# A two-layer decoder step on one core: the recurrence in another order and in other PSUM banks, and the first norm's root multiplied in behind the projection

## The chip, the cores and the metric

The kernel runs on one core of a Trainium2 chip. The time is device microseconds from the start of one execution to its end. Three runs of the kernel before took 1614.56 to 1616.03 us, with a median of 1615.8. The profile is of one further execution, which took 1614.58 us.

## What is computed

The reference runs two decoder layers for 512 prompt tokens and 8 sample tokens (520 columns in all, 1024 features). The change touches the first half of layer 0:

```python
proj = rms_norm(x, norm_g) @ w_in            # 1024 -> 3600 columns
qkv, gdn_conv = causal_conv(g_qkv, ...)      # width 4, then silu; the same for x/B/C of the SSD heads
q, k = l2_normalize(q), l2_normalize(k)
beta = sigmoid(g_b);  g = -exp(A_log) * softplus(g_a + dt_bias)      # the gates
# chunks, 4 delta-rule heads:
lower = strict(kb @ k.T * decay);  u, w = solve(eye + lower, [v*beta, kb*exp(cum)])
v_new = u - w @ S;  o = (q*exp(cum)) @ S + (q @ k.T * decay) @ v_new
S = S * exp(last) + (k * exp(last - cum)).T @ v_new
# chunks, 8 SSD heads:  scores = C B^T * seg;  y = scores @ x + (C * exp(cum)) h;  h updated likewise
```

rms_norm multiplies each token by the inverse root of its mean square, and each feature by a gain. Behind the recurrence follow a second norm, the output projection, an FFN, and layer 1 (latent attention with a paged cache, and another FFN). These are as they were.

## The kernel before

**Layout.** Everything lies with features on the 128 partitions and tokens along the row, so x is 8 tiles of 128 x 520 (`xres`). Large products are done with the operands split in two parts, high and low: of the activations `xnh` and `xnl`, of the weights `wsplit` halves made by ScalarE (`high`, L1126) and VectorE (`low`, L1563) from a ring of four slots that SP fills, 512 KB each. An output tile takes for each of 8 feature tiles six matmuls of 260 columns (high with high, high with low, low with high, in two column halves). Tiles go to two pairs of PSUM banks in turn (0 and 1, 2 and 3). `gemm_ready` says that a tile is done, `tile_taken` that it has been read out, and the tile after the next one waits for that and for its weights (`w_split`).

**Start.** SP issues x in two DMAs, the page table, and then the weights. GpSimd issues the constants (1280 KB), the gains and six small tensors. When x and the page table are there, ScalarE squares the 8 tiles (L1109), VectorE adds them (L1518, L1521), TensorE sums over partitions (`norm_sum`), ScalarE makes the inverse root with an Ln and an Exp (L1113, L1115). Then for each tile VectorE forms the normalized x (`xraw`, L1617), ScalarE copies its high part (L1197), VectorE takes the low part (L1621), and TensorE follows tile by tile.

**Projection.** 28 output tiles in 7 turns of four. The first 20 go through the convolution. For each, ScalarE makes the high half of the weights of the tile after next, copies the tile from PSUM (L1207, two small copies for the outputs behind it) and, after VectorE's convolution, applies SiLU (L1215). VectorE makes the low half, then one multiply (L1633) and three rounds of multiply-add (L1636, L1638). Turn 0 stands by itself and turns 1 to 4 are a loop on every engine. Each engine runs its list in order, so a SiLU that waits for the convolution also holds ScalarE's next high half. After turn 0 TensorE does the gates: 40 matmuls of 16 columns from the normalized x and `wgate`, which VectorE and ScalarE turn into decays with about 15 small operations. The last 8 tiles (z) are copied out by ScalarE (L1246) into `hid`, between the lengths of q and k. ScalarE then applies SiLU to all eight z tiles in one operation (L1260).

**Recurrence.** Four chunks of 128 tokens. TensorE's list for a chunk: 12 decay sums broadcast over partitions into banks 0 to 2 (`cumB_mm`; 4 delta heads, 8 SSD heads), beta (bank 3), key-key (4), key-query (5), transposes of k (6) and v (7), then for the SSD part B-C products (0) and transposes of x (1) and B (2), then the first mask product transposed (3, `xinit_mm`). ScalarE makes exponentials of the sums (L1269, L1270). VectorE waits for them, subtracts each token's own sum (12 operations, L1699), waits for ScalarE's exponential (L1272), forms `bm` and `lt` (L1704, L1707), `attnt` (L1709), `xinvt` and `xinv` (L1711, L1713) and the scaled k and v (L1716 to L1719, `kvs_ready`). GpSimd multiplies `lt` with 7 masks (L435), each for one level of the inversion. Six levels follow: two products `y` (one for each half of the heads, copied by ScalarE, L1282), and two products that VectorE subtracts from `xinv` and `xinvt` (L1758, L1760). After level 0 VectorE does the SSD scores and the two state queries `ce` (L1726 to L1733); TensorE's SSD outputs behind level 1 wait for both. After the levels come `w_mm` (copied by ScalarE, L1284), `vnew_mm` (L1286), the outputs and the state products, and VectorE's state update (L1769). In the trace these transposes and matmuls appear as one or two records each, nearly all under the helper's line L505.

Of the kernel before, what the change touches and what calls it, by code (L numbers as in the profile page):

```python
# [57 lines left out]
INV_BANKS = ((3, 4, 5), (6, 7, 2))  # L58
# [12 lines left out]
SMALLS = ['w_gate', 'gains', 'convw', 'convb', 'small', 'gatec', 'prev']  # L71
# [32 lines left out]
def build(nc, A, O):  # L104
    ctx = ExitStack()
    with ctx:
# [22 lines left out]

        xraw = hid[:, 20:28]  # L130
# [142 lines left out]
        spt = sqsum[:, 0:256]  # L273
        rqs, qr, krn = sb("rqs", 128, 4, MH), sb("qr", 128, ROUNDS, 32), sb("krn", 128, ROUNDS)
# [7 lines left out]
        def unit(n):  # L282
# [3 lines left out]
        x_loaded, c_loaded, g_loaded = sem("x_loaded"), sem("c_loaded"), sem("g_loaded")  # L286
# [13 lines left out]
            w_mm w_ready qe_ready vnew_ready ot_mm ot_taken kv_mm s_ready bc_mm xtm_mm btm_mm score_ready  # L300
            xdt_ready btm_ready ce_ready yt_mm yt_taken hup_mm h_ready rec_stored st_loaded
            sprep_ready spread_mm spread_ready rhs2_ready sv_mm vnt_ready qks_mm row_mm row_ready
            sel_mm sel_taken y0_mm xds_ready hsel_mm hsel_taken s_decayed osq_ready osq_mm
            mix_ready dve_own h0_loaded ln_ready rinv_ready big_stored out_stored
            w_hi w_split part_done xn_raw xn_hi hid_hi hid_ready mix_split silu_ready up_ready
# [45 lines left out]
        def _(sp_):  # L351
            for k in range(2):
                sp_.dma_start(xres[:, 4 * k:4 * k + 4], A['x'][:, 4 * k:4 * k + 4]).then_inc(x_loaded, 16)
            sp_.dma_start(ptab[:, :], A['page_table']).then_inc(x_loaded, 16)
# [9 lines left out]

            def pages():

                sp_.wait_ge(x_loaded, 48)
# [14 lines left out]
            for stage, turns, _ in STAGES:  # L382
                for u in range(4):
# [4 lines left out]
                    load(stage, 0, u)  # L388
# [21 lines left out]
        def _(pool):  # L410
            pool.dma_start(cst[:, :, :], A['consts']).then_inc(c_loaded, 16)
            for dst, src in zip((wgate, gains, convw, convb, small, gatec, prev), SMALLS):
                pool.dma_start(dst[:], A[src]).then_inc(g_loaded, 16)
# [68 lines left out]
            pool.wait_ge(x_loaded, 48)  # L482
# [20 lines left out]
        def _(pe):  # L503
# [9 lines left out]
            def split_gemm(stage, high, low, begin=0, end=None, norm=None, after=None, ready=None):  # L513
# [45 lines left out]
            def norm_sum(n):  # L559
                pe.wait_ge(s('sq_added'), (KD - 1) * (n + 1))  # L560
# [5 lines left out]
            pe.wait_ge(c_loaded, 16)  # L566
            norm_sum(0)

            split_gemm('proj', xnh, xnl, 0, 1, norm=0)

            pe.wait_ge(g_loaded, 16 * len(SMALLS))
# [36 lines left out]
            for c in range(NCH):  # L608
# [14 lines left out]
                if c:  # L623
                    pe.wait_ge(s('x_ready'), 2 * LV * c)
# [1615 lines left out]
```

## Time and profile before

| | |
|---|---|
| median of 3 runs | 1615.8 us |
| profiled execution | 1614.58 us, its span 1612.9 us |
| busy: TensorE / its weight loads | 1526.5 us (95%) / 1424.2 us (88%) |
| busy: VectorE / ScalarE / GpSimd | 743.0 us (46%) / 604.6 us (37%) / 159.6 us (10%) |
| mean granted TensorE clock | 0.97 |
| chain that ended last, by engine | TensorE 89%, VectorE 5%, ScalarE 3% |

Start to 34 us is the norm and the first tile, to 209 us the projection, to 397 us the four chunks. In the rows, times are microseconds from the start of the span, the second figure is the time that the piece or instruction takes, and brackets hold the engine's idle time ahead of it with what ended it. A granted clock of 1.00 is 2.4 GHz and of 0.50 is 1.2 GHz.

### The profile page before, as it was taken

To read this page: it belongs to the slowest core of one execution; us is meant where nothing else is said; L and a number is where in the kernel's file an instruction comes from. 1 tells how busy PE (TensorE), PEld (TensorE's weight loads), DVE (VectorE), ACT (ScalarE), POOL (GpSimd) and SP (SyncE) were. 2 spreads that over 40 slices of the span, in tenths; PEclk is the share of its full clock that TensorE was granted. 3 is DMA by queue.
4 is the path that set the end of the run, shared out by engine and by line. 5 is a ranking of instruction groups with operands and counts; after the bars stand their busy time and mean duration, and the time that the engine had idled before them with its cause. 6 is when DMAs were issued, how large, how long until landed. Compare 5 with 4: busy or idle time off the path is not lost.

```text
span 1612.9 us, 29294 instructions
## 1 busy us (share of the span) xinstructions
PE 1526.5 (95%) x11912; PEld 1424.2 (88%) x11912; DVE 743.0 (46%) x1243; ACT 604.6 (37%) x934; POOL 159.6 (10%) x192
## 2 busy tenths in 40 slices
PE   4999978888799999999999999999899999999999
PEld 4999977777588999999999967677799999999998
DVE  5577346565574444444323425455434444444222
ACT  4454632221523443442222363456524443442111
POOL 1000022211160000000010000252111000000000
PEclk9999989898899999999999999999889999999999
DMA  5223200002134323333332322264322323332332
GB/s 185 68 80 103 69 11 1 1 1 104 49 77 162 90 89 94 91 90 104 91 95 78 96 78 79 71 179 145 131 79 81 92 90 92 92 90 89 94 95 76
DMA packets 46274, 140.27 MB, mean 87 GB/s; under 512 B 6706, under 2 KB 16018, under 8 KB 45042
## 3 DMA queue, kind: packets, MB, share of 16 engines
q1 hardware_dynamic: 39842, 114.38, 23.5%
q0 software_dynamic: 6064, 20.60, 4.3%
q10 hardware_dynamic: 288, 4.19, 0.7%
q8 instruction: 54, 0.88, 0.2%
q14 instruction: 26, 0.21, 0.0%
HBM read 130.34 MB, written 7.76 MB: 86 GB/s over the span
## 4 chain that ended last, share of the span: by engine, by line
PE 89%; DVE 5%; ACT 3%; issue 1%; DMA 1%; POOL 0%; SPq 0%; DVEq 0%; ACTq 0%
PE PS L505 88%; PE PS L971 1%; DVE arena L1699 1%; DMA ptab<-in_page_table 1%; DVE arena L1726 0%; POOL arena L435 0%; DVE arena L1617 0%; ACT rinv L1113 0%; DVE xnl L1621 0%; DVE sqsum L1521 0%; ACT arena L1452 0%; ACT arena L1260 0%; DVE arena L1760 0%; DVE arena L1955 0%; ACT sq L1319 0%
## 5 line engine op out<-in xcount | busy, mean ns | idle before, releaser
L505 PE MATMUL PS<-xnh,wsplit 128*128 128x260 f32 x3904 | 637.5, 285 | 7.0 <-DVE xnl L1621 4.4
L505 PEld LDWEIGHTS PS<-xnh,wsplit 128*128 128x128 f32 x3904 | 541.2, 190 | 9.3 <-issue 7.7
L505 PE MATMUL PS<-xnl,wsplit 128*128 128x260 f32 x1952 | 394.6, 284 | 0.0
L1126 ACT ACTIVATE wsplit<-wring 128x1024 fp32r<-128x1024 f32 x176 | 182.8, 1041 | 464.3 <-PE PS L505 457.9
L1563 DVE TENSOR_TENSOR wsplit<-wring,wsplit 128x1024 fp32r<-128x1024 f32 x176 | 211.0, 1201 | 247.1 <-ACT wsplit L1126 247.0
L505 PEld LDWEIGHTS PS<-xnl,wsplit 128*128 128x128 f32 x1952 | 302.3, 190 | 0.0
L505 PE MATMUL PS<-arena 128*128 128x128 f32 (+4 forms) x1328 | 209.3, 329 | 24.7 <-DVE arena L1699 5.6
L505 PE MATMUL PS<-hidh,wsplit 128*128 128x260 f32 x1408 | 226.6, 283 | 0.0
L505 PEld LDWEIGHTS PS<-arena 128*128 128x128 f32 (+2 forms) x1328 | 173.7, 207 | 58.2 <-issue 24.5
L505 PEld LDWEIGHTS PS<-hidh,wsplit 128*128 128x128 f32 x1408 | 192.9, 188 | 0.0
L505 PE MATMUL PS<-hidl,wsplit 128*128 128x260 f32 x704 | 141.3, 282 | 0.0
L505 PEld LDWEIGHTS PS<-hidl,wsplit 128*128 128x128 f32 x704 | 108.7, 188 | 0.0
L1577 DVE TENSOR_TENSOR sq<-PS,rinv 128x520 f32<-128x520 f32 x44 | 30.8, 700 | 119.9 <-PE PS L505 119.9
L1582 DVE TENSOR_TENSOR sgate<-PS,rinv 128x520 f32<-128x520 f32 x44 | 30.8, 700 | 119.3 <-PE PS L505 105.6
L505 PE MATMUL PS<-sq,cst 128*128 128x260 f32 (+1 forms) x184 | 51.7, 416 | 7.6 <-ACT sq L1319 6.7
L1126 ACT ACT_TABLE_LOAD x24 | 30.8, 1283 | 70.2 <-PE PS L505 70.1
L1282 ACT ACTIVATE arena<-PS 128x256 f32<-128x256 f32 x48 | 18.5, 384 | 92.0 <-PE PS L505 91.4
L435 POOL TENSOR_TENSOR arena<-arena,cst 128x512 f32<-128x512 f32 x28 | 36.3, 1329 | 166.9 <-DVE arena L1707 166.9
L505 PEld LDWEIGHTS PS<-sq,cst 128*128 128x128 f32 (+1 forms) x184 | 27.6, 164 | 22.3 <-ACT sq L1319 10.0
L422 POOL TENSOR_TENSOR sqsum<-sqsum,sq 128x520 f32<-128x520 f32 x18 | 32.9, 1826 | 126.2 <-ACT sq L1109 125.8
L1638 DVE SCALAR_TENSOR_TENSOR arena<-arena,convw 128x512 f32<-128x512 f32 x60 | 44.8, 747 | 0.0
L1452 ACT ACTIVATE arena<-PS,nb,rqs 128x512 f32<-128x512 f32 (+1 forms) x64 | 38.8, 628 | 1.9 <-DVE nb L2005 1.9
(356 smaller groups left out, 1645.9 us busy)
## 6 DMA issues: line engine op xcount, KB each, us to landing
wring<-in_w_gu SPq DMA_DIRECT2D x88, 512.0 KB, 3.6
wring<-in_w_dn SPq DMA_DIRECT2D x32, 512.0 KB, 3.5
wring<-in_w_proj SPq DMA_DIRECT2D x28, 512.0 KB, 3.6
wring<-in_w_dn SPq DMA_DIRECT2D x16, 384.0 KB, 3.2
wring<-in_w_outa SPq DMA_DIRECT2D x8, 512.0 KB, 3.7
wring<-in_w_inc SPq DMA_DIRECT2D x8, 512.0 KB, 3.6
wring<-in_w_uq SPq DMA_DIRECT2D x8, 512.0 KB, 4.8
wring<-in_w_outc SPq DMA_DIRECT2D x8, 512.0 KB, 3.8
```

Source lines behind the costliest of these rows:

```text
L422: pool.tensor_tensor(sqsum[:, :], sqsum[:, :], sq[:, k % 2, :], ALU.add).then_inc(s('sq_added'), 1)
L435: pool.tensor_tensor(by(mt[:, l], GH), by(lt, GH), across(const(f'inv{l}'), GH), ALU.mult)\
L505: return pe.matmul(out, lhsT, rhs, start=start, stop=stop)
L971: ins = pe.transpose(PS[:, bank(h, e), at_:at_ + 128], pm[:, PLACE[q] + kb * 128:PLACE[q] + (kb + 1) * 128], ident)
L1126: act.activation(dst[:, 0:w], wring[u][:, 0:w], ACT.Copy).then_inc(s('w_hi'), 1)
L1282: act.activation(yinv[:, hs_], PS[:, by_, hs_], ACT.Copy).then_inc(s('y_ready'), 1)
L1452: ins = act.activation(pm[:, to:to + w], PS[:, b0 + e, at_:at_ + w], ACT.Exp, bias=nb[:, q:q + 1], scale=rqs[:, q, h:h + 1], accum_out=den ...
L1563: tt(wl[:, 0:w], wring[u][:, 0:w], wh[:, 0:w].bitcast(F32), ALU.subtract).then_inc(s('w_split'), 1)
L1577: tt(two(supt), bank2(2), two(root), ALU.mult).then_inc(tile_taken[1], 1)
L1582: tt(two(sgate[:, q, :]), bank2(0), two(root), ALU.mult).then_inc(tile_taken[0], 1)
L1638: st(stt(out=cacc[:, p, 0:T], in0=raw[:, p, t:t + T], scalar=w(t), in1=cacc[:, p, 0:T], op0=ALU.mult, op1=ALU.add), s('conv_done') if t == ...
L1699: st(stt(out=arg[:, h // 4, hs_], in0=PS[:, h // 4, hs_], scalar=cumt[:, c, h:h + 1], in1=const('decaymask'), op0=ALU.subtract, op1=ALU.mi ...
```

## The change

**First norm.** x comes in four DMAs with a semaphore each, the first weights right behind the first of them, and the page table goes to GpSimd's list. GpSimd issues the gains first and the constants and small tensors only when the second quarter of x is there. ScalarE makes `xnh` as x times the gain, squares between, and VectorE makes `xnl` (`gained_low`) with the adds of the squares between. `norm_sum(0)` stands behind tile 0 on TensorE. Its root goes to `sqsum`, and VectorE multiplies with it as it reads each of the 28 tiles out of PSUM; ScalarE's copies of them are gone and its two small output copies read `raw`. The gates take raw x with `wgate` times the gain, and five matmuls of one column turn the root for them, which VectorE multiplies in.

**Recurrence.** The decay sums are in two groups, the four delta heads first. VectorE no longer waits for an exponential ahead of the first arguments; the other eight arguments stand behind `lt`, four on each side of `xinvt`. Key-key and key-query of the next chunk stand behind `w_mm` and `vnew_mm` of this one. The v transposes go to bank 2 behind the y products of level 0, the transposed B to bank 0 beside the B-C products, the second half's banks change from (6, 7, 2) to (7, 6, 2). Each `ce` has its own signal. Some semaphores are merged (`osq` into `l2`, `qks` into `spread`) with the counts to suit.

```diff
             for k in range(4):
+                sp_.dma_start(xres[:, 2 * k:2 * k + 2], A['x'][:, 2 * k:2 * k + 2]).then_inc(x_loaded[k], 16)
+                if k == 0:
+                    load('proj', 0, 0)
...
+            pool.dma_start(gains[:], A['gains']).then_inc(s('gains_loaded'), 16)
+            pool.wait_ge(x_loaded[1], 16)
             pool.dma_start(cst[:, :, :], A['consts']).then_inc(c_loaded, 16)
...
-                up(0, norm, (lambda: norm_sum(norm)) if norm in (1, 3) else None)
+                up(0, norm, (lambda: norm_sum(norm)) if norm in (0, 1, 3) else None)
...
+            for k in range(KD):
+                act.wait_ge(x_loaded[k // 2], 16)
+                act.activation(xnh[:, k, :], xres[:, k, :], ACT.Copy, scale=gains[:, 0, k:k + 1]).then_inc(s('xn_hi'), 1)
+                if k:
+                    square(0, k - 1, (x_loaded[(k - 1) // 2], 16))
+                if k == 1:
+                    high('proj', 0, 0)
...
+                    dve.wait_ge(gemm_ready[p], i * 2 + (u // 2 + 1))
+                    tt(two(raw[:, p, 3:3 + TOK]), bank2(2 * p), two(sqsum[:, :]), ALU.mult).then_inc(tile_taken[p], 1)
                     low('proj', i if u < 2 else i + 1, (u + 2) % 4)
...
+                decay_args(range(GH), s('arg_ready'))
                 dve.wait_ge(s('dect_ready'), 2 * c + 1)
...
+                dve.wait_ge(s('cumB_mm'), 2 * c + 2)
+                dve.wait_ge(s('ecum_ready'), 2 * c + 2)
+                decay_args(range(GH, 2 * GH))
                 dve.wait_ge(s('mt_ready'), (LV + 1) * c + 1)
                 st(tt(by(xinvt, GH), ident4, by(mt[:, 0], GH), ALU.subtract))
+                decay_args(range(2 * GH, NDEC), s('arg_ready'))
...
                 ins.then_inc(s('w_mm'), 1)
+                if c + 1 < NCH:
+                    key_key(c + 1)
...
                 ins.then_inc(s('vnew_mm'), 1)
+                if c + 1 < NCH:
+                    key_query(c + 1)
```

## Rows read from the trace of the kernel before

**Rows 1.** The chain that ended last, in order of time, the start (start, us, what).
```profile
17.85 3.82 PE PS L505 x8
...
26.60 0.67 DVE arena L1617
27.88 0.67 DVE arena L1617
...
33.06 176.07 PE PS L505 x1428
```

**Rows 2.** The timeline of the start (start, us, engine, line, operation).
```profile
11.78 1.84 ACT L1109 ACTIVATE sq<-xres 128x520 f32<-128x520 f32 x3 [9.60 <-DMA ptab<-in_page_table]
...
34.95 1.06 ACT L1126 ACTIVATE wsplit<-wring 128x1024 fp32r<-128x1024 f32 x1 [1.88 <-PE PS L505]
```

**Rows 3.** DMA issues (count, size, us to landing), then one stretch of the windows view.
```profile
wring<-in_w_proj SPq DMA_DIRECT2D x28, 512.0 KB, 3.6
...
cst<-in_consts POOLq DMA_DIRECT2D x1, 1280.0 KB, 10.6
...
gains<-in_gains POOLq DMA_DIRECT2D x1, 16.0 KB, 10.0
...
4.00:5.00 1.00, 0.00 (x0) 0.00 (x0) 0.00 (x0) 0.00 (x0) 1.00 (x3) 1.00 1.01 408
```

**Rows 4.** The timeline of the gates on TensorE.
```profile
52.00 8.27 PE L505 MATMUL PS<-wgate,arena 128*128 128x16 f32 x62
```

**Rows 5.** The timeline of the convolution loop, ScalarE's rows, then VectorE's.
```profile
115.07 0.73 ACT L1215 ACTIVATE arena<-arena,convb 128x520 f32 x1 [3.79 <-DVE arena L1638]
...
117.12 1.06 ACT L1126 ACTIVATE wsplit<-wring 128x1024 fp32r<-128x1024 f32 x1
...
140.18 1.06 ACT L1126 ACTIVATE wsplit<-wring 128x1024 fp32r<-128x1024 f32 x1
...
118.21 1.23 DVE L1563 TENSOR_TENSOR wsplit<-wring,wsplit 128x1024 fp32r<-128x1024 f32 x1 [3.30 <-ACT wsplit L1126]
...
122.96 1.22 DVE L1563 TENSOR_TENSOR wsplit<-wring,wsplit 128x1024 fp32r<-128x1024 f32 x1
```

**Rows 6.** The costliest groups of instructions: the FFN's evictions (busy us, mean ns).
```profile
L1577 DVE TENSOR_TENSOR sq<-PS,rinv 128x520 f32<-128x520 f32 x44 | 30.8, 700 | 119.9 <-PE PS L505 119.9
```

**Rows 7.** The timeline of the first chunk's end and the second's beginning.
```profile
256.02 2.94 PE L505 MATMUL PS<-arena 128*128 128x128 f32 x24 [0.69 <-ACT arena L1286]
...
258.85 2.92 PE L505 MATMUL PS<-cst,la 128*128 128x128 f32 x24
259.00 1.12 DVE L1769 SCALAR_TENSOR_TENSOR arena<-arena,PS 128x128 f32<-128x128 f32 x4 [6.83 <-PE PS L505]
...
262.29 1.02 ACT L1270 ACTIVATE arena<-PS 128x1024 f32<-128x1024 f32 x1
...
262.50 1.13 DVE L1699 SCALAR_TENSOR_TENSOR arena<-PS,cumt,cst 128x128 f32<-128x128 f32 x4 [2.38 <-ACT arena L1269]
...
263.66 0.63 ACT L1272 ACTIVATE arena<-arena 128x512 f32<-128x512 f32 x1 [0.35 <-DVE arena L1699]
...
266.47 0.69 DVE L1707 TENSOR_TENSOR arena<-PS,arena 128x512 f32<-128x512 f32 x1
...
267.24 9.08 POOL L435 TENSOR_TENSOR arena<-arena,cst 128x512 f32<-128x512 f32 x7 [36.51 <-DVE arena L1707]
268.54 1.74 DVE L1711 TENSOR_TENSOR arena<-cst,arena 128x512 f32<-128x512 f32 x1 [0.78 <-POOL arena L435]
...
270.20 0.68 DVE L1713 TENSOR_TENSOR arena<-cst,PS 128x512 f32<-128x512 f32 x1
...
272.73 7.01 PE L505 MATMUL PS<-arena 128*128 128x128 f32 x44 [1.09 <-DVE arena L1719]
...
281.06 0.45 PE L505 MATMUL PS<-arena,sq 128*64 128x128 f32 x4 [1.32 <-DVE sqsum L1733]
```

**Rows 8.** One stretch: busy PE, PEld, DVE, ACT, POOL, granted clock, DMA share, GB/s.
```profile
222.00:224.00 2.00, 1.03 (x5) 1.03 (x6) 1.22 (x2) 0.31 (x1) 2.00 (x2) 0.50 0.00 0
```

More of the change, by code:

```diff
@@ L387, in _ @@
                         sp_.wait_ge(*slot_freed(before, TURNS[before] - 1, u))
-                    load(stage, 0, u)
+                    if before or u:
+                        load(stage, 0, u)
                 if stage in ('inc', 'uq', 'dn0', 'dn1'):
@@ L679, in _ @@
                         pe.wait_ge(s('y_ready'), 2 * (LV * c + l) + half + 1)
+                        if l == 0 and half:
+                            pe.wait_ge(s('kvs_ready'), 2 * c + 2)
                         if l < LV - 1:
@@ L1610, in ffn, with square_added @@
                     gained_low(2, KD - 1)
-            for u in range(2):
-                low('proj', 0, u)
-            dve.wait_ge(s('rinv_ready'), 1)
-            for k in range(KD + 1):
-                if k < KD:
-                    st(stt(out=xraw[:, k, :], in0=xres[:, k, :], scalar=gains[:, 0, k:k + 1], in1=rinv[:, 0, :],
-                           op0=ALU.mult, op1=ALU.mult), s('xn_raw'))
-                if k:
-                    dve.wait_ge(s('xn_hi'), k)
-                    st(tt(xnl[:, k - 1, :], xraw[:, k - 1, :], xnh[:, k - 1, :].bitcast(F32), ALU.subtract), s('xn_ready'))
+            def square_added(k):
+                dve.wait_ge(s('sq_ready'), k + 1)
+                if k == 0:
+                    st(dve.tensor_copy(sqsum[:, :], sq[:, 0, :]), s('sq_added'))
+                else:
+                    dve.wait_ge(s('sq_added'), k)
+                    st(tt(sqsum[:, :], sqsum[:, :], sq[:, k % 2, :], ALU.add), s('sq_added'))
+            for k in range(KD):
+                gained_low(0, k)
+                if k == 1:
+                    low('proj', 0, 0)
+                if k:
+                    square_added(k - 1)
+            low('proj', 0, 1)
+            dve.wait_ge(c_loaded, 16)
+            dve.wait_ge(g_loaded, 16 * len(SMALLS))
+            st(tt(wgate[:, :, :], wgate[:, :, :], over(gains[:, 0, :], NGATE), ALU.mult), s('gprep_ready'))
+            dve.wait_ge(s('rinv_ready'), 1)
             def conv_turn(i, first):
@@ L1673, in _ @@
             st(dve.tensor_copy(cumt[:, :, :], PS[:, 7, 0:NCH * NDEC].rearrange("p (c n) -> p c n", n=NDEC)), s('cumt_ready'))
-            for z in range(6):
-                low('proj', (22 + z) // 4, (22 + z) % 4)
+            for z in range(8):
+                dve.wait_ge(gemm_ready[z % 2], 10 + z // 2 + 1)
+                tt(two(hid[:, TZ + z, :]), bank2(2 * (z % 2)), two(sqsum[:, :]), ALU.mult).then_inc(tile_taken[z % 2], 1)
+                if z < 6:
+                    low('proj', (22 + z) // 4, (22 + z) % 4)
                 for j in (2 * z - 2, 2 * z - 1) if 1 <= z <= 4 else ():
@@ L1732, in ssd_scores @@
                     for g in range(SG):
[L1733 to L1734 removed]
+                        state_query(g)
                 def ssd_out():
```

226 lines of the change are left out of this document (111 added, 115 removed).

## The prediction

> **What bounds the kernel now.** I read the page first: TensorE is busy nearly throughout, and the chain that ended last lies on it for nine tenths. So only a stretch in which TensorE waits, or works at its lower clock, can give time back. The chain in order of time has two such stretches. The first is the start: until 33 us it runs through a DMA, ScalarE, VectorE and the sum of squares, and from 33.06 it is TensorE alone for 176 us [rows 1]. ScalarE sits idle 9.60 us until all of x and the page table have landed, and the first tile of the projection ends, to be seen by the ACT row that waits for it, at 34.95 [rows 2]. The second is the recurrence, four chunks of some 45 us, each beginning with a ladder of short waits between engines before the six levels of the inversion [rows 7]. Between them lies the projection: no PE wait, so what is taken from ScalarE there gives nothing, and what is added to VectorE may cost.
>
> **Part 1, the start.** Removed: the wait for the norm before the first matmul. xnh and xnl are made from x times the gain as each quarter of x lands, the sum of squares goes behind tile 0, and its root is multiplied in at each eviction. A is the time at which the first quarter of x (520 KB) and the gains are there. A weight load of 512 KB lands 3.6 us after its issue, and the queues move 408 GB/s early on [rows 3]; with issue in the first microsecond, A is 5.0 by estimate. Bounds: 4.5, and 11 if the gains, now first on their queue, still took the 10.0 us that they took behind the constants [rows 3].
> From A: two copies to xnh and one square (0.6 each by the squares, three in 1.84 [rows 2]), then the high half of the weights, 1.06 [rows 5]: A+2.9. Its low half on VectorE, 1.23 [rows 5]: TensorE starts at A+4.1. After the first add (0.4) VectorE does one three-operand and one two-operand pass for each further k, as before with other operands, where a pair came every 1.28 us [rows 1]: six more pairs, the last add at A+12.2, tile 0 ends beside it. Then the sum of squares: 3.82 us at the start of the kernel before [rows 1], half that if the clock is up by then. In the kernel before the same pace of work brought it up within tile 0, so 1.9: tile 1 begins at A+14.3, its weights being split by A+13.4. That is 19.3 against 34.9: **15.6 us gained** (9.6 to 16.1). The constants, 1280 KB issued only when the second quarter of x has landed (about 7 us), are wanted at A+12.3 = 17.3; before they took 10.6 us from issue, beside all of x [rows 3]. That is just enough; each microsecond later costs one.
>
> The gates use raw x now, and five one-column matmuls more turn the root: 8.27 us for forty such [rows 4] is 0.21 each, **1.1 lost**. The few small VectorE operations on the roots (some 0.9 us) lie beside the first tile of the next turn, which lasts over 5 us.
>
> **Part 2, eviction on VectorE.** ScalarE loses a 0.6 us copy a tile, which nobody waits for. VectorE gets 0.70, by the same shape in the FFN [rows 6]. Is there room? In the loop a turn takes VectorE 4.75 us (122.96 less 118.21) and four tiles 23.06 (ACT's 117.12 to 140.18) [rows 5]. The cycle that binds is VectorE and ScalarE together: three turns (14.25), the fourth up to the end of its convolution (4.85), SiLU and a table load to the next high half (115.07 to 117.12, 2.05, and 0.1 of waking) and that half (1.1): 22.35, or 0.7 under TensorE. The eviction of the first tile falls in VectorE's wait for ScalarE (3.3 us at 118.21 [rows 5]); the other three add 1.9 to 2.1, so 24.3, 1.2 over. What is late next is the low half that VectorE makes after the first eviction: TensorE needs it one tile (5.8) after that tile, it comes 4.7 after in the kernel before, so 1.1 us of delay is free. Queued behind that half on VectorE is the convolution, for which only ScalarE's SiLU waits. The first two of four rounds use the slack up, the last two and the boundary behind the loop pay: **2.0 lost** (0 to 5). The last eviction before the recurrence is 0.1 slower than ScalarE's.
>
> **Part 3, the recurrence.** Times are from the start of the output matmuls of the chunk before, 256.02 [rows 7]. Before: these and the state products end at 2.9, all twelve decay sums follow (2.92), ScalarE makes an exponential that VectorE waits for, then all twelve arguments, then bm and lt; lt ends at 267.16, or 11.1. After: only the first four decay sums (a third of 2.92) up to 3.9; VectorE is through the state update (1.12) at 4.1, four arguments 1.13, exponential 0.63, bm and lt 1.5 with the waits: 7.5. GpSimd starts there, its first mask product takes 1.3 (7 in 9.08), so 8.85. VectorE meanwhile waits for the 1.02 us exponential of the last two banks (end about 8.0), makes four arguments (9.25), then xinvt. [Rows 7] show that this one takes 1.74 against 0.68 for its like with one operand in PSUM, beside GpSimd; I take it as 10.9. The last four arguments read PSUM and one table, like the 0.68 kind, so 12.0 and xinv 12.7 (at 1.0 more if they stretch as xinvt does, at 1.0 less if xinvt does not). TensorE needs the last arguments for banks 0 and 1 (1.3 of products and transposes, to 13.3), two y products (1.0) and the v transposes moved here (0.5): first update products at 14.85. Before, the second y began at 16.7 and the update products at 17.2 [rows 7]: 2.35 gained a chunk (1 to 3.5). The query products begin after the first of two ce operations and not the second: TensorE waited 1.32 there [rows 7], 0.6 gained. The key products moved behind w_mm and vnew_mm are a third of 2.92 each, 0.98, in waits of 0.69 [rows 7]: 0.3 lost twice, in three chunks. The first chunk, whose arguments waited for the same exponential, is taken alike. Sum 4 x 2.95 - 3 x 0.6 = **10.0 gained** (4 to 17).
>
> The stretching in rows 7 has a rule. The Trainium skill (SBUF — State Buffer, "SBUF: two separate sides") says that a VectorE operation with two SBUF inputs and a GpSimd operation that reads SBUF hold a shared port in turn, the other blocked for the whole instruction. The 1.74, about one mask product's remainder longer than 0.69, agrees, and by the rule the moved arguments are free of it.
>
> **Sum.** 15.6 - 1.1 - 2.0 - 0.1 + 10.0 = 22.4. The profiled execution took 1614.6 (span 1612.9), 1.2 under the median of 1615.8; so 1592.2 on its scale and about 1593 on that of the median.
>
> **Rivals.**
> *The clock stays up in the recurrence.* Now it falls to 0.50 (1.2 GHz) where TensorE waits often: in 222 to 224 it is busy 1.03 of 2.0 us [rows 8], and the level that begins at 272.73 needs 7.01 us for 44 records, 0.16 each against 0.12 in the 24 at 258.85 [rows 7]. Shorter ladders may spare that, 1.5 us a chunk: 1587. Against it: new waits at 7.5 to 8.9 and 10.0 to 12.0. 0.13.
> *The recurrence gives it back.* The ladder's new waits let the clock fall earlier, and products that now run at 0.12 a record take twice that: some twenty records a chunk on the chain, 2.4 us. Then part 3 brings nothing and 1603 is left. For it: the same row of 222 to 224 [rows 8]. 0.12.
> *The constants come late.* GpSimd issues them while VectorE works without a pause until A+13.4; if they land only 6 us after that, tile 1 begins 6 later: 1599. Against: beside GpSimd in [rows 7] only xinvt is stretched, xinv is not, and GpSimd's issues come before VectorE's longest passes. 0.08. The Trainium skill (same page and section) has the mechanism: VectorE in a mode with both ports keeps GpSimd from writing DMA descriptors; no row before shows the two together.
> *Slower.* VectorE becomes the projection's bound by so much that the clock falls between tiles. A tile of 5.8 us would take up to 11.5. At four tiles in this state the gain is gone, at twenty the kernel takes 1700. It decides if a turn of VectorE is longer than 5.8 by several tenths more than 4.75 + 0.70. Against: the sum above stays a few tenths a tile over TensorE, and TensorE would still be busy nine tenths, not one half as in rows 8. 0.03.
> *It does nothing*, the first matmul waiting for something else as late: 0.02.
>
> **Chances and range.** Forecast, gains from 16 to 27 us: 0.62; its own range 1588 to 1600. The range 1584 to 1604 takes in the clock cases on both sides and late constants, and leaves out under 2 in 10. A difference of 0.2% (3.2 us) is what the runs can tell from none. Faster by more: 0.95; within: 0.02; slower: 0.03.
>
> **What would show it.** First xnh copy near 5 us, tile 1 beginning near 19; the ACT row behind the first tile at 17 to 20, where 34.95 stands. PE waits of about a microsecond in the loop's late rounds, none in the first. lt some 7.5 us after the output matmuls, the chunk's period 42 us. Wrong would be a first matmul after 12 us, a projection longer by over 5 us, or chunks still of 44 us or more.

## The result, and the profile after

The changed kernel takes 1588.1 us (median of four runs, 1586.04 to 1594.2); the kernel before, on the same chip, 1615.18 us. The ratio is 0.9837, with a 95% interval of 0.9822 to 0.9852. The forecast was 1593, with a range of 1584 to 1604. The profiled executions have spans of 1587.1 and 1612.9 us, 25.8 apart, and this is where the 25.8 lie:

| stretch | gained, us | predicted |
|---|---|---|
| start, to the second tile's row on ScalarE (40.66 to 26.05) | 14.6 | 15.6 |
| gates (9.2 to 12.55) and the first microseconds behind them | -3.7 | -1.1 |
| projection's loop and end | -2.3 | -2.1 |
| recurrence | 14.9 | 10.0 |
| the samples' stretch behind it (code hardly changed) | 2.6 | 0 |
| all that follows | -0.4 | 0 |

**The start.** The chain of waits in order of time, from the changed kernel (start, us, what):

```profile
1.41 4.51 DMA gains<-in_gains
5.95 1.35 ACT xnh L1215 x2
...
17.50 40.58 PE PS L509 x296
```

It now begins with a DMA of 16 KB, and from 17.50 it is TensorE alone, which answers to 33.06 in [rows 1]. ScalarE's row behind the second tile, and what the constants took from issue to landing in the first 16 us:

```profile
26.05 1.07 ACT L1149 ACTIVATE wsplit<-wring 128x1024 fp32r<-128x1024 f32 x1 [3.20 <-PE PS L509]
```
```profile
cst<-in_consts POOLq DMA_DIRECT2D x1, 1280.0 KB, 9.2
```

The constants, 10.6 before [rows 3], are there when TensorE wants them: its sum of squares stands at 18.33, behind tile 0 without a wait.

**The gates.** TensorE's timeline, then two stretches of the windows view (busy PE, PEld, DVE, ACT, POOL, granted clock, DMA share, GB/s):

```profile
37.38 1.85 PE L509 MATMUL PS<-wgate,xres 128*128 128x16 f32 x16
...
41.57 3.57 PE L509 MATMUL PS<-wgate,xres 128*128 128x16 f32 x16
...
49.75 0.19 PE L509 MATMUL PS<-cst,sqsum 128*8 128x1 f32 x2
```
```profile
36.00:40.00 4.00, 4.00 (x38) 4.00 (x36) 3.31 (x6) 1.87 (x4) 0.00 (x0) 1.00 0.27 104
...
44.00:48.00 4.00, 4.00 (x21) 4.00 (x20) 0.00 (x0) 1.35 (x2) 0.00 (x0) 0.50 0.00 0
```

The same sixteen records take 1.85 and 3.57 us. The clock fell although the profile has TensorE busy 4.00 of 4.00 us.

**The loop.** ScalarE's first high half of two turns, then VectorE's low halves inside one:

```profile
107.97 1.06 ACT L1149 ACTIVATE wsplit<-wring 128x1024 fp32r<-128x1024 f32 x1
...
132.19 1.06 ACT L1149 ACTIVATE wsplit<-wring 128x1024 fp32r<-128x1024 f32 x1
```
```profile
114.42 1.22 DVE L1573 TENSOR_TENSOR wsplit<-wring,wsplit 128x1024 fp32r<-128x1024 f32 x1
119.79 1.21 DVE L1573 TENSOR_TENSOR wsplit<-wring,wsplit 128x1024 fp32r<-128x1024 f32 x1
```

A turn takes 24.22 where it took 23.06 [rows 5], and VectorE needs 5.37 a tile instead of 4.75. TensorE, which had no wait in the loop before, now has one of 0.38 us at 110.34 and this one a turn later:

```profile
134.56 0.51 PE L509 MATMUL PS<-xnh,wsplit 128*128 128x260 f32 x2 [0.89 <-DVE wsplit L1573]
```

**The recurrence.** VectorE's timeline of the second chunk from the state update on, then TensorE's first update and query products:

```profile
247.07 1.12 DVE L1810 SCALAR_TENSOR_TENSOR arena<-arena,PS 128x128 f32<-128x128 f32 x4 [6.83 <-PE PS L509]
...
250.72 0.69 DVE L1742 TENSOR_TENSOR arena<-PS,arena 128x512 f32<-128x512 f32 x1
...
252.89 1.64 DVE L1749 TENSOR_TENSOR arena<-cst,arena 128x512 f32<-128x512 f32 x1
254.45 1.11 DVE L1730 SCALAR_TENSOR_TENSOR arena<-PS,cumt,cst 128x128 f32<-128x128 f32 x4
255.49 0.67 DVE L1752 TENSOR_TENSOR arena<-cst,PS 128x512 f32<-128x512 f32 x1
```
```profile
259.86 5.18 PE L509 MATMUL PS<-arena 128*128 128x128 f32 x40
265.76 0.45 PE L509 MATMUL PS<-arena,sq 128*64 128x128 f32 x4 [0.72 <-DVE rinv L1735]
```

In [rows 7] the state update is at 259.00, lt at 266.47, xinv at 270.20, the query products at 281.06. Counted from the state update, lt comes 3.65 us behind it instead of 7.47, xinv 8.42 instead of 11.20, the query products 18.69 instead of 22.06. A chunk's period can be read from ScalarE's copy that follows the transposes, four times in the changed kernel and four times before:

```profile
215.63 0.39 ACT L1297 ACTIVATE rinv<-PS 128x256 f32<-128x256 f32 x1 [0.61 <-PE PS L668]
...
257.02 0.38 ACT L1297 ACTIVATE rinv<-PS 128x256 f32<-128x256 f32 x1 [0.26 <-PE PS L668]
...
298.41 0.39 ACT L1297 ACTIVATE rinv<-PS 128x256 f32<-128x256 f32 x1 [0.47 <-PE PS L668]
...
339.73 0.39 ACT L1297 ACTIVATE rinv<-PS 128x256 f32<-128x256 f32 x1 [0.61 <-PE PS L668]
```
```profile
221.92 0.38 ACT L1277 ACTIVATE rinv<-PS 128x256 f32<-128x256 f32 x1 [0.55 <-PE PS L651]
...
267.29 0.38 ACT L1277 ACTIVATE rinv<-PS 128x256 f32<-128x256 f32 x1 [0.32 <-PE PS L651]
...
311.84 0.38 ACT L1277 ACTIVATE rinv<-PS 128x256 f32<-128x256 f32 x1 [0.33 <-PE PS L651]
...
357.21 0.39 ACT L1277 ACTIVATE rinv<-PS 128x256 f32<-128x256 f32 x1 [0.33 <-PE PS L651]
```

41.39, 41.39 and 41.32 us, against 45.37, 44.55 and 45.37. This copy lies in the ladder, where the clock moves, so its place shifts with the clock. Where the clock matters, a chunk is taken between two of ScalarE's copies of the output products (L1288 before, L1308 after), which stand at the chunk's end. Three such chunks in the windows view, two of the kernel before and one of the changed kernel (length, busy times, granted clock in the third place from the end):

```profile
258.10:302.66 44.56, 36.90 (x296) 33.88 (x295) 26.39 (x61) 10.09 (x22) 9.08 (x7) 0.96 0.00 1
302.66:348.03 45.37, 39.23 (x296) 36.19 (x295) 26.48 (x61) 10.09 (x22) 9.08 (x7) 0.89 0.01 1
```
```profile
246.18:287.36 41.18, 36.19 (x296) 33.88 (x295) 26.22 (x61) 10.08 (x21) 9.10 (x7) 0.96 0.00 1
```

The chunk after these two took 45.18 us at 0.92 in the kernel before. The changed kernel's other two took 41.18 and 41.15, both at 0.96. The profiles below are compared by these copies ("the chunks"), by the table load that opens the recurrence (at 201.24 us in the changed kernel, "the table load"), and by the table load behind the first FFN's last turn (732.18 against 758.36). From the last output copy to ScalarE's first root behind the samples ("the samples' stretch") it took 22.19 us before and 19.55 after. TensorE's second group of large products there, before and after:

```profile
406.44 3.18 PE L505 MATMUL PS<-arena 128*32 128x512 f32 x16
```
```profile
381.56 1.92 PE L509 MATMUL PS<-arena 128*32 128x512 f32 x16
```

The stretch from the end of the first FFN to the second FFN's first table load, the attention, is the same code in every kernel here and took 477.8 us after and 477.4 before.

### The profile page after: what moved, and what is told of

Its sections match the earlier page's. It is cut to its first block, busy times and chain, and to the rows that moved or that the text cites. A ratio compares the mean times of both kernels' runs of the same rounds, so it can differ in the third digit from the quotient of the medians.

```text
span 1587.1 us, 29335 instructions
## 1 busy us (share of the span) xinstructions
PE 1519.4 (96%) x11922; PEld 1420.7 (90%) x11922; DVE 755.2 (48%) x1268; ACT 593.4 (37%) x906; POOL 160.3 (10%) x193
## 4 chain that ended last, share of the span: by engine, by line
PE 86%; DVE 6%; ACT 3%; issue 3%; DVEq 0%; DMA 0%; POOL 0%; ACTq 0%; POOLq 0%
PE PS L509 84%; DVE arena L1662 1%; PE PS L994 1%; DVE arena L1730 0%; ACT wsplit L1149 0%; DVE arena L1657 0%; DVE arena L1652 0%; DVE arena L1768 0%; DVE wsplit L1573 0%; DVE arena L1749 0%; DMA gains<-in_gains 0%; ACT arena L1472 0%; ACT rinv L1136 0%; DVE arena L1801 0%; ACT arena L1281 0%
## 5 line engine op out<-in xcount | busy, mean ns | idle before, releaser
L509 PE MATMUL PS<-xnh,wsplit 128*128 128x260 f32 x3904 | 638.1, 285 | 14.2 <-DVE wsplit L1573 11.3
L509 PE MATMUL PS<-arena 128*128 128x128 f32 (+4 forms) x1328 | 199.6, 316 | 14.5 <-DVE arena L1730 6.6
L509 PEld LDWEIGHTS PS<-arena 128*128 128x128 f32 (+2 forms) x1328 | 166.6, 199 | 45.1 <-issue 25.0
```

Of the source, the lines that this page charges most:

```text
L509: return pe.matmul(out, lhsT, rhs, start=start, stop=stop)
```

## The experiments

Each of these twelve was timed in five rounds beside the kernel before. E1 to e9, and e11, start from the changed kernel or the one before; e10 and e12 put together what the others pointed to.

**The halves apart.** E1 is the kernel before with the new norm and projection only, e2 the kernel before with the new recurrence only.

```
e1: every hunk of the diff except INV_BANKS and the loop over c
e2: INV_BANKS and the loop over c alone
```

> The kernel before with the changed first norm and projection alone; the recurrence keeps its old order, old banks and one signal. If the two halves of the change are worth what the two traces show them to be worth in their own places (14.6 us at the start, 3.4 lost in the gates, 2.3 in the projection's loop, 0.4 in its end), this runs 8.6 us faster than before: 1606.6 us, and its four chunks take 44.5 to 45.4 us each, as before. If the recurrence owes part of its gain to something that the new start brings (a clock that recovers elsewhere), the chunks are shorter than that and the time is below 1604. By the prediction's terms (15.6 - 1.1 - 2.0 - 0.1 = 12.4) it would be 1602.8.

> The kernel before with the changed recurrence alone; start, gates and projection as before. If the new order alone gives the shorter chunks and the shorter stretch behind them, this runs 14.9 + 2.6 = 17.5 us faster than before, 1597.7 us, with chunks of 41.2 us and the turned rows of the sample stretch at 1.92 us a group instead of 3.18. If the 2.6 us behind the recurrence came by chance of the clock, 1600.3 us; if the prediction's price for the recurrence holds (10.0), 1605.2 us.

E1 took 1605.15 us, ratio 0.9934 (0.9921 to 0.9948); e2 1599.9 us, 0.9900 (0.9884 to 0.9916). E1's chunks are 44.64, 45.18 and 44.60 us, so the start does nothing for the recurrence; e2's are 41.19, 40.24 and 41.37, so the new order alone shortens them. The product of the two ratios is 0.9835, the whole change's is 0.9837: the halves add up. E2 came out between 1597.7 and 1600.3; in its profile the samples' stretch took 22.16 us, as long as before (22.19), so the new order alone does not bring the 2.6 us there. E1's profile also holds a test of the clock in the old order. Its first chunk between output copies:

```profile
248.25:293.43 45.18, 38.23 (x296) 35.16 (x295) 26.38 (x61) 10.09 (x22) 9.07 (x7) 0.92 0.01 1
```

The other two took 44.60 and 44.66 us, both at 0.96. With the kernel before, the old order took 44.56 to 44.66 at 0.96, 45.18 at 0.92 (twice) and 45.37 at 0.89: the clock costs up to 0.8 us a chunk there. In the new order e2's chunks took 39.53 and 39.54 at 1.00 and 42.07 at 0.92. At one and the same clock the new order is 3.4 us (0.96) or 3.1 us (0.92) shorter.

**The place of the root's matmuls.** E3 moves the five one-column matmuls behind the forty.

```diff
-                ins = mm(PS[..., 5 * NGATE + t:...], sqsum[:, toks], ident[:, 0:1])   (in the loop over t)
+            for t in range(5):
+                ins = mm(PS[..., 5 * NGATE + t:...], sqsum[:, toks], ident[:, 0:1])
```

> The changed kernel with one edit: the five one-column matmuls that turn the root stand behind the forty gate matmuls and no longer between their groups. Theory: the forty-five small matmuls cost 12.5 us instead of 9.15 because the clock falls to half at 41 us, four microseconds into them, and the place of the five does not matter: 12.3 to 12.7 us again, no change of the time. Rival: the five alternate stationary shapes and break the stream, and it is they that bring the clock down early: then the gates take about 9.2 + 5 x 0.3 = 10.5 us and the kernel is 2 us faster, 1586 us.

1588.57 us, 0.9837 (0.9823 to 0.9852): the time of the changed kernel. TensorE's rows are

```profile
37.84 9.18 PE L509 MATMUL PS<-wgate,xres 128*128 128x16 f32 x80
46.94 1.99 PE L509 MATMUL PS<-cst,sqsum 128*128 128x1 f32 x10
```

11.1 us in all, less than expected and near the rival's 10.5. It is not the edit's doing: e1 and e4, with the gates as in the changed kernel, took 11.4 and 11.3 in their profiles, e10 13.7, and e2, with the old gates, 11.13 for the eighty records that took 9.22 in the profile before. The clock falls somewhere in this run of small matmuls, earlier or later. The price of the five cannot be read from the difference of two such profiles.

**One signal for both ce products.** E4 undoes the split.

```diff
-  s('ce_ready'))                      +  s('ce_ready') if g else None)
-  if h % 4 == 0: wait 2 * c + h // 4 + 1      +  if h == 0: wait c + 1
```

> The changed kernel with one edit: VectorE signals once for both ce products, and TensorE waits for both before the first group of the state products, as before. Prediction's term: the split is worth 0.6 us a chunk, so this is 2.4 us slower, 1590.5 us. Rival: TensorE's group waits for other work anyway and nothing moves, 1588.1 us. Second rival: the later start lets the clock fall for longer in the ladder behind it, and it costs over 4 us.

1591.09 us, 0.9852 (0.9836 to 0.9868), 3.0 more than the changed kernel; chunks 42.16, 41.58 and 41.99 us, 0.54 more on the mean. TensorE's wait ahead of the second chunk's query products, 0.72 us in the changed kernel, is 1.32 again, as in [rows 7]:

```profile
264.99 0.45 PE L509 MATMUL PS<-arena,sq 128*64 128x128 f32 x4 [1.32 <-DVE sqsum L1735]
```

Between output copies and at one clock e4 is 0.4 to 0.6 us longer: 41.58 against 41.18 (0.96), and against e2 42.70 to 42.07 (0.92) and 40.13 to 39.54 (1.00). The term of 0.6 was right.

**The gates between the tiles.** E5 issues them behind tiles 2 to 4 of the first turn.

```diff
+            def gate_tiles(u):
+                for t in ((), (0, 1), (2, 3), (4,))[u]: ...   (called behind tile u)
```

> The changed kernel with one edit: the gate matmuls and the turned root are issued two token groups at a time behind the second, third and fourth tile of the projection's first turn, and no longer in one piece of 11 to 12.5 us between the first turn and the loop. Theory: the clock falls in that piece because forty-five small matmuls follow each other, and between big tiles it stays at 1.00; then the groups take about 9.3 us together, the 2 to 3 us that they lost come back, and so do the first microseconds of the loop at .50: 3 to 5 us faster, 1583 to 1585 us. Rival: the clock falls behind every pair of groups as well, and each fall costs part of the big tile after it: no gain, or up to 4 us slower. Second rival: the groups fill time in which TensorE waits for VectorE's evictions of the first turn anyway, and the gain is over 6 us.

1591.74 us, 0.9853 (0.9835 to 0.9872). The first rival was right: the groups themselves ran at 1.85 and 1.94 us, and the clock fell behind each pair, inside the next big tile (windows of e5; the first groups stand at 26.01 and 27.93, and 24 to 28 us has 1.00):

```profile
32.00:36.00 4.00, 4.00 (x26) 4.00 (x26) 0.18 (x1) 0.00 (x0) 0.00 (x0) 0.69 0.02 7
```

The table load is at 200.63, no earlier than in e1, e3 and e4 (199.66 to 200.15). What the profile has above the changed kernel's lies in the attention (480.6 us).

**The first tap on ScalarE.** E6 takes 0.66 us a tile from VectorE.

```diff
+   act.activation(cacc[:, p, :], raw[:, p, 3:3 + TOK], ACT.Copy, scale=first_tap(i * 4 + u))
-   st(ts_(cacc[:, p, :], raw[:, p, 3:3 + TOK], w(3), None, ALU.mult))
```

> The changed kernel with one edit: the convolution's first product (raw times the fourth tap) is made by ScalarE behind its wait for the multiplied tile, and VectorE starts with the second tap. Theory: the projection's loop is bound by VectorE since it took the eviction over (24.22 us a turn against 23.06), and 0.66 us less per tile takes it below TensorE: the turn goes back to about 23.1 us, 2.3 us (at most 4 x 1.16 = 4.6) faster in all, 1584 to 1586 us. Rival: VectorE now waits for ScalarE's product and the turn stays at 24.2 or grows: 1588 us or more.

1588.79 us (1584.06 to 1592.8), 0.9819 (0.9800 to 0.9838). ScalarE's first high half of two turns:

```profile
106.18 1.06 ACT L1149 ACTIVATE wsplit<-wring 128x1024 fp32r<-128x1024 f32 x1
...
129.25 1.06 ACT L1149 ACTIVATE wsplit<-wring 128x1024 fp32r<-128x1024 f32 x1
```

The turn is 23.07 us again, and TensorE has no wait left in the loop. From ScalarE's first high half behind the gates to the table load e6 took 139.97 us, the changed kernel 141.77 (e11, the same kernel again, 141.74): 1.8 of the theory's 2.3. At the end of the first FFN it is 2.1 ahead of the changed kernel's first profile and 0.9 ahead of e11. But its span is 4.0 longer, because the attention took 483.9 us instead of 477.8. One group of 32 records, the changed kernel's and e6's:

```profile
1010.51 4.00 PE L509 MATMUL PS<-qkn,arena 128*128 128x16 f32 x32
```
```profile
1009.27 6.85 PE L509 MATMUL PS<-qkn,arena 128*128 128x16 f32 x32
```

The code is the same. These are again small matmuls, and the clock had fallen earlier: the eight records ahead of them took 3.33 us in e6 and 2.43 in the changed kernel. In the profiles of all runs the attention took 477.4 to 477.9, 480.6, 482.3 or 483.9 us.

**Filled waits.** E7 puts fourteen matmuls of constants a chunk into TensorE's waits.

```diff
+   if c: wait s_ready                                               (ahead of the first seven)
+   for _ in range(7): mm(PS[:, 7, 0:128], ident, const('triu'))    (ahead of the wait for mt)
+   for _ in range(7): mm(PS[:, 7, 0:128], ident, const('triu'))    (ahead of the wait for xinit_ready)
```

> The changed kernel with one edit: seven matmuls of constants into an unused bank in each of TensorE's two waits at the beginning of a chunk (for the inverted block, and for the first inverse), 14 of about 0.21 us a chunk; their result is read by nobody. Theory: the clock stands at .52 to .62 for four microseconds of each chunk because TensorE waited 1.8 and 1.7 us just before; filled, it stays at 1.00, the 26 matmuls in 256 to 260 us take 2.6 us instead of 4, and a chunk is 1 to 1.4 us shorter: 4 to 6 us, 1582.5 to 1584 us. Rival: the ladder behind is bound by the copies between matmuls and not by the clock, and nothing moves. Second rival: the filling outlasts the waits and costs up to 1 us a chunk.

1594.77 us, 0.9863 (0.9843 to 0.9882): slower than the changed kernel. Its profile, though, reaches the end of the first FFN at 732.32, 0.1 us behind the changed kernel; what it has beyond that is an attention of 483.9 us, which its edit doesn't touch. Its chunks are 42.72, 41.10 and 41.11 us. Five microseconds around the second chunk's copy, the changed kernel first, then e7, and TensorE's rows of e7:

```profile
255.50:260.50 5.00, 4.79 (x28) 4.82 (x29) 2.89 (x6) 2.32 (x5) 5.00 (x5) 0.66 0.00 0
```
```profile
255.00:260.00 5.00, 3.72 (x33) 3.75 (x34) 3.53 (x9) 1.77 (x4) 5.00 (x5) 1.00 0.00 0
```
```profile
256.28 0.68 PE L509 MATMUL PS<-arena 128*128 128x128 f32 x4 [1.74 <-DVE arena L1736]
...
257.46 1.73 PE L509 MATMUL PS<-cst 128*128 128x128 f32 x14
259.02 1.06 PE L509 MATMUL PS<-arena 128*128 128x128 f32 x8
```

The clock stayed at 1.00, as the theory had it. What it saved went to my placing of the second filling: TensorE waits ahead of the bc products (1.74 us, still unfilled), not behind the transposes, and there the filling held up the y products, which start at 259.02 and not behind 257.46. Between output copies e7's chunks are 41.11 us at 1.00, where e2 has 39.54 at 1.00: the filling cost 1.6 us, about what the clock gave. The second rival was right, with more than its 1 us, and the first fails against e8 and e12.

**Keys back.** E8 puts both key products back into the chunk's own beginning.

```diff
-   if c == 0: key_key(0)                  +   if c: wait x_ready;   key_key(c)
-   if c + 1 < NCH: key_key(c + 1)             (behind w_mm; key_query alike)
```

> The changed kernel with one edit: the key-key and key-query products of every chunk stand at that chunk's own beginning, as before, and no longer in the end of the chunk before. The prediction priced their place in the end at 0.6 us a chunk and their absence from the beginning as part of 2.35. If the end's copies hide them (the trace shows the copies 2.74 us apart in both kernels), moving them back gains nothing there; at the beginning TensorE has 1.8 us of wait, so theory: 0 to 0.9 us a chunk slower in three chunks, 1588 to 1591 us. Rival by the prediction's own price: 0.6 faster in the end, against a loss at the beginning of 0.9: 1589 us as well, but the chunk's end then shows copies 0.6 us closer together.

1590.74 us, 0.9834 (0.9819 to 0.9848). The chunks are 41.41, 40.60 and 39.55 us. The first, at the clock of the changed kernel, has its length (41.41 against 41.39). Between output copies e8's chunks are 41.20 at 0.96, where the changed kernel has 41.18, and 39.56 and 39.55 at 1.00, where e2 has 39.53 and 39.54: the key products cost nothing at either place, and the term of 0.3 for each was wrong. The other two show something else. The five microseconds around its second, third and fourth copy:

```profile
255.00:260.00 5.00, 4.53 (x26) 4.57 (x27) 2.89 (x7) 2.31 (x5) 5.00 (x5) 0.66 0.00 0
295.60:300.60 5.00, 3.93 (x33) 3.82 (x34) 4.54 (x11) 2.21 (x5) 5.00 (x5) 1.00 0.00 0
335.20:340.20 5.00, 3.98 (x34) 3.87 (x35) 4.54 (x11) 2.21 (x5) 5.00 (x5) 1.00 0.01 3
```

The chunk of 40.60 lies between the copies at 257.02 (0.66) and 297.62 (1.00); the chunk between 297.62 and 337.17, with 1.00 at both, took 39.55. In the new order the clock counts.

**VectorE's order undone.** E9 makes all twelve decay arguments ahead of bm and lt.

```diff
+   wait cumB_mm, ecum_ready; kdarg; decay_args(range(GH, NDEC), s('arg_ready'))     (ahead of bm)
-   ... decay_args(range(GH, 2 * GH))  and  decay_args(range(2 * GH, NDEC), ...)      (behind lt)
```

> The changed kernel with one edit: VectorE makes all twelve decay arguments of a chunk ahead of the product that feeds the ladder, as before, and no longer eight of them behind it; TensorE and ScalarE keep the new order. Theory: this order on VectorE is the greater part of what a chunk gained; the ladder's first inverse stands 2.8 us later against the state update than in the changed kernel (11.2 against 8.4 us behind its start), so a chunk takes about 44.2 us instead of 41.4 and the kernel is 11 us slower, 1599 us. By the prediction's term it would be 2.35 a chunk: 9.4 us, 1597.5 us. Rival: the shorter chunk came from the earlier transposes and keys on TensorE and from the clock, and VectorE's order is worth under 1 us a chunk: 1592 us or less.

1602.08 us, 0.9916 (0.9902 to 0.9929), 14 us slower; chunks 44.49, 44.44 and 44.40 us, near those of the kernel before. VectorE's rows of its second chunk:

```profile
248.15 1.12 DVE L1809 SCALAR_TENSOR_TENSOR arena<-arena,PS 128x128 f32<-128x128 f32 x4 [6.83 <-PE PS L509]
...
252.85 0.17 DVE L1739 TENSOR_TENSOR arena<-PS,cumt 128x12 f32<-128x12 f32 x1 [2.54 <-ACT arena L1292]
...
259.98 0.69 DVE L1751 TENSOR_TENSOR arena<-cst,PS 128x512 f32<-128x512 f32 x1 [0.39 <-PE PS L509]
```

Xinv is 11.83 us behind the state update, 0.6 worse than before: VectorE now waits 2.54 us for the exponential of banks 1 and 2, which the new order of TensorE and ScalarE has put late. So this is not the price of VectorE's order alone. Between output copies e9's chunks are 44.39 to 44.43 us at 0.92, where the old order has 45.18 and e2 42.07: the new order of TensorE and ScalarE with the old order of VectorE is worth 0.8 us a chunk, of which the split ce signal has 0.4 to 0.6, and VectorE's order on top of it 2.3.

**The same kernel again, and the better versions.** E11 is the changed kernel without an edit. E10 takes e6's tap, brings the gains by ScalarE's own queue and fills TensorE's wait behind the recurrence.

```diff
+   act.dma_start(gains[:], A['gains'])              -   pool.dma_start(gains[:], A['gains'])
+   for _ in range(11): mm(PS[:, 5, 128:256], ident, const('triu'))   (ahead of sprep_ready)
```

> The changed kernel once more, without an edit. It tells how far the times of one kernel lie apart: theory: chunks of 41.2 to 41.4 us again, since every chunk begins alike, but the stretch behind the recurrence at 49.5 or 51.2 us and the attention's beginning at 477.8 or 480 to 484 us by where the clock falls in them, so 1587 to 1592 us. Rival: the order of this kernel fixes those two as well, and both come out as in its first profile (49.5 and 477.8 us).

> The changed kernel with three edits that aim at what it left: ScalarE makes the convolution's first product (2 us in the loop), the gains come by ScalarE's own queue instead of GpSimd's (ScalarE waited for them until 5.95 us; up to 1.3 us if the first quarter of x is there before them), and eleven matmuls of constants fill TensorE's wait of 2.5 us behind the recurrence (the sample stretch then runs at 1.00; 1 to 2 us). Theory: the attention's start is 4 to 5 us earlier than in the changed kernel, and 1583.5 us where the clock of the attention's beginning is the same; up to 6 us of that can be lost there, where equal code took 477.4 to 483.9 us in the profiles so far. Rival: x is no earlier than the gains and the filling only delays: 1586 to 1588 us.

E11: 1588.19 us (1587.46 to 1595.64), 0.9843 (0.9822 to 0.9863). The chunks are 41.39, 41.38 and 41.37; the samples' stretch took 20.53 us where the first profile had 19.55 and the kernel before 22.19, and the attention 477.73. E1, with the old recurrence, took 20.96 there, and e2, e5 and e8, with the new one, 22.16. So the 2.6 us behind the recurrence go with the profile and not with the order. In e11 TensorE also waits 0.52 us there for the load of `in_s_ssm` (2048 KB from GpSimd's queue), which took 9.9 us from issue to landing and 9.0 in the first profile, without a wait. E10: 1584.34 us (1581.58 to 1586.55), 0.9808 (0.9794 to 0.9822). The gains land sooner:

```profile
5.00 1.35 ACT L1217 ACTIVATE xnh<-xres,gains 128x520 fp32r<-128x520 f32 x2 [2.39 <-DMA gains<-in_gains]
```

The attention starts 4.9 us earlier than in the changed kernel's first profile (727.26 against 732.18), in spite of gates that took 13.7 us. E10 is 3.9 us under e11, its companion on that chip, and its five runs all lie below e11's five. In the profiles it is 3.7 ahead of e11 at the attention's start; 1.4 of that came in the chunks, two of which ran at 1.00, which no edit of e10 touches.

E12 is e10 with e7's fillings (and its wait for s_ready), the second now ahead of the wait for the last decay arguments.

```diff
+   for _ in range(7): mm(PS[:, 7, 0:128], ident, const('triu'))   (ahead of the wait for mt)
+   for _ in range(6): mm(PS[:, 7, 0:128], ident, const('triu'))   (ahead of the wait for ecum_ready, arg_ready)
```

> The kernel of e10_together with the filling of the chunk's beginning put right: seven matmuls of constants in TensorE's first wait, as in e7_filled_gaps, and six in its second, now ahead of the wait for the last decay arguments instead of behind the transposes, where TensorE did not wait and the fourteen records (1.73 us) held up the first y products. Theory: e7_filled_gaps had the clock at 1.00 in the ladder's beginning and lost its worth to its own misplaced filling, so this one has chunks of 39.5 to 39.9 us instead of 41.2 and runs 4 to 6 us faster than e10_together: 1578 to 1580.5 us. Rival: the clock in the ladder's beginning is worth nothing (the chain there is the copies), and chunks stay at 41 us: 1584 us. Second rival: what the chunks gain is lost again where the clock falls later, in the attention's beginning.

A chunk between output copies, and TensorE's second group of large products in the samples' stretch:

```profile
241.18:280.72 39.54, 37.44 (x322) 35.18 (x321) 26.21 (x61) 9.97 (x21) 9.11 (x7) 1.00 0.00 1
```
```profile
372.58 3.64 PE L508 MATMUL PS<-arena 128*32 128x512 f32 x16 [2.47 <-DMA arena<-in_s_ssm]
```

The chunks are 39.55 us each by the copy behind the transposes, at the low end of the theory. The time does not show it: 1586.99 us, five runs at 1578.65, 1580.14, 1586.99, 1587.66 and 1587.71, ratio 0.9795 (0.9770 to 0.9821). At its fourth copy (330.77) the profiled one is 5.3 us ahead of e10, at the end of the first FFN (725.04) 2.2. TensorE came to the sixteen records above before `in_s_ssm` had landed, waited 2.47 us (e10 1.30), and they took 3.64 us, 1.92 in e10. Then the attention took 483.9 us, 6.4 more than in e10. The theory held for the chunks and the second rival for the attention; a load that no term named took the rest. The intervals of e10 and e12 end at 0.9822 and 0.9821, where those of the changed kernel begin (0.9822, twice). For e10 the runs beside e11 bear it out; e12 was timed on another chip, and three of its five runs lie in the changed kernel's range. That e12 is faster than e10 is not shown.

## Why the prediction was right, and where its terms were not

**The start: right, one microsecond off.** 14.6 against 15.6. At tile 1's beginning the gain is 15.06 by the prediction's own count (34.95 less 19.89); the other 0.45 lies between that and ScalarE's row behind the tile. A was 5.95 and not 5.0, because the gains came last. Once they came by another queue it was 5.00. The pace behind A was as worked out: the sum of squares at A+12.4 (worked out: A+12.2), tile 1 at 19.89, or A+13.9 (A+14.3). The rival of late constants did not happen: they took 9.2 us. The Trainium skill (SBUF — State Buffer, "SBUF: two separate sides") says that VectorE in a mode with both ports keeps GpSimd from writing DMA descriptors. VectorE worked from 6.71 on, GpSimd issued the constants at 7.46, and no hold-up shows; whether any of VectorE's operations ran in such a mode no row tells.

**The gates: mis-sized.** -1.1 was reckoned at the rate of [rows 4], as if that were the rate of this work. (The 8.27 us there are 62 records and not all forty matmuls; all eighty records took 9.22, which makes the term 1.15.) The rate is a mixture of two clocks: the profile before has 1.00 until 56 us and 0.50 from 58, and e2 took 11.13 for the same work. At 1.00 one of the five holds the next group up by 0.23 us (39.08 to 39.31), at 0.50 by 0.43 (44.98 to 45.41). With the new gates the piece took 12.55 us in the profile after and 10.7 to 13.7 in those of the experiments.

**VectorE's eviction: right.** A turn of 24.22 was forecast as 24.3, the loss as 2.0 and measured as 2.3; e6 took the cause away, got the 23.06 back and with it 1.8 of the 2.3.

**The recurrence: right in mechanism, 4.9 too small.** Counted from the state update, the query products were to come 2.95 us earlier (2.35 for the ladder, 0.6 for ce) and came 3.37 earlier: 4 x 0.42 = 1.7. The key products cost nothing instead of 0.6 in three chunks: 1.8. The remaining 1.4 are in the third and fourth chunk, which I took as alike: there the kernel before ran at 0.89 and 0.92 and took 0.8 and 0.6 us more than at 0.96, and the changed kernel has 0.96 in both.

Inside the ladder the 3.37 have three parts. VectorE's first subtraction of level 0 comes 13.60 us behind the state update (260.67) instead of 15.84 (274.84): 2.24, where the ladder's 2.35 was worked out. From it to the scores (277.11 before, 262.41 after) another 0.53 is gained, and in the wait for ce 0.60. Two errors lie within the first part. Xinv ended 9.09 us behind the beginning of the state update (255.49 and its 0.67), where the prediction's 12.7 is 9.7 on that count. It stood directly behind the last four arguments, as worked out; they took 1.11 us and were not stretched beside GpSimd, while xinvt, with both operands in SBUF, was (1.64). That agrees with the rule of the Trainium skill (SBUF — State Buffer, "SBUF: two separate sides") that the prediction cites. The update products, though, came 12.79 us behind the state update and not 11.9, with TensorE at a mean clock of 0.66 just then; in e12, at 1.00, they came 11.15 behind it. In the kernel before they were late as well, which the 17.2 read from [rows 7] left out.

**The rival that named the time.** "The clock stays up in the recurrence" gave 1587 and the kernel takes 1588.1, but it gave only the 1.4 us just named. The clock still falls in the changed kernel, to a mean of 0.96 in each chunk between output copies, for some four microseconds: 41.18 us, where 39.54 is left without that (e12, and e8's third chunk by the copy). From 0.96 to 0.92 the old order loses 0.6 us a chunk and the new one 0.8 to 1.0 (e2, e5, e10). No profile has an old chunk at 1.00, so what the clock costs there in all is not shown.

**What no term held.** 2.6 us came behind the recurrence. There the same sixteen records of 512 columns took 1.92 us in the changed kernel, and in the kernel before 3.18. By e2, e5 and e8, which have the new order and 22.16 us for this stretch, the 2.6 are no property of the new order.

**Luck in the sum.** Term by term the forecast missed by -1.0 (start), -2.6 (gates), -0.2 (projection), +4.9 (recurrence), +2.6 (samples) and -0.4 (the rest). Only 3.3 of these 11.7 us are left in the sum, and that the errors cancelled so far is luck.

What stays open is why the clock falls early or late in the same code. These runs show where, and what it costs.

## What to carry to other kernels

Read the granted clock beside every duration from which a cost is extrapolated: a row of small matmuls may be an average over two rates. A wait on TensorE costs twice, in itself and in the lower clock behind it, and here the second part was 1.6 us a chunk; filling it with work that nobody reads paid only in the very place of the wait (e12 against e7), and part of what it gained was lost at the next bound, a load. Measure a repeated piece between points where the clock is the same: a marker inside the slow stretch put 0.6 us of the clock's cost into the wrong chunk here (e1). When a time moves by less than the runs of one kernel lie apart (8 us here), compare profiles at a checkpoint before the stretch that varies.

## What the runs showed of the hardware

- TensorE's clock fell to 0.50 while its rows were busy without a gap: matmuls of 16 columns, 37 to 50 us, 1.85 us for sixteen records at one level and 3.57 at the other.
- Chunks of the new order took 39.53 to 39.56 us at a mean granted clock of 1.00 (e2, e5, e8, e10, e12), 40.98 to 41.20 at 0.96 (after, e3, e6, e8, e11) and 41.98 to 42.16 at 0.92 (e2, e5, e10).
- The load of `in_s_ssm` (2048 KB, GpSimd's queue) took 9.0 us from issue to landing (after, e10) to 10.2 (e12).
- Identical code took 477.4 to 483.9 us in the attention, and the whole kernel 1587.46 to 1595.64 us in five runs (e11).
- A load of 16 KB landed at 5.9 us from GpSimd's queue, issued at 1.41, and by 5.0 from ScalarE's, issued at 0.88 (e10).
